# Attention stages of a streaming encoder on one core: sample values once per pair of heads, query squares one head at a time, and the weight split at the pair's end

## The reference, cut to what matters

```python
q = (rms_norm(c_q, q_lat_norm[l]) @ w_uq[l]).reshape(B, L, N_HEADS, QK_DIM)      # 16 heads x 96
q = jnp.concatenate([q[..., :NOPE_DIM], apply_rope(q[..., NOPE_DIM:], pos)], axis=-1)
q = rms_norm(q, q_head_norm[l])
k_nope = (ckv_all @ w_uk[l]).reshape(B, T, N_HEADS, NOPE_DIM)
k = rms_norm(jnp.concatenate([k_nope, kr_all (broadcast to heads)], axis=-1), k_head_norm[l])
v = (ckv_all @ w_uv[l]).reshape(B, T, N_HEADS, V_DIM)
att_out = blocked_attention(q, k, v, pos, k_pos)        # chunk-causal softmax(q k') v
mixed = sigmoid(g_rec) * rec_out + sigmoid(g_att) * att_out
```

## Time and profile before

| | |
|---|---|
| median of 3 runs | 3244.86 us (3240.8 to 3248.27) |
| the profiled execution | 3247.03 us, its span 3245.3 us |
| mean granted TensorE clock | 0.91 of full speed |
| attention, layer 0 and layer 1 | about 430 to 740 us and 1925 to 2245 us of the span |
| DMA, all queues | 119 GB/s over the span |

### The profile page before, as it was taken

One profiled execution on the slowest core, in us unless ns is written; L12 is line 12 of the kernel. 1 busy time (PEld: TensorE's weight loads), 2 busy tenths in 40 slices (PEclk: granted clock), 3 DMA queues, 4 the chain that ended last, 5 costly groups with the idle time before them and its releaser, 6 DMA issues.

```text
span 3245.3 us, 43898 instructions
## 1 busy us (share of the span) xinstructions
PE 2862.5 (88%) x18152; PEld 2624.5 (81%) x18152; DVE 2019.5 (62%) x3294; ACT 1380.2 (43%) x1938; POOL 315.7 (10%) x457
## 2 busy tenths in 40 slices
PE   2998789999798999999789969998888969999996
PEld 2988678888787999999789958887877958888884
DVE  4666666664554443434577567665545368988997
ACT  1334156553333221212333336654333347777773
POOL 3000023330000000000000023221000010000001
PEclk9999789887788999999899979888879889999998
DMA  4322200002131222222122210001212179999995
GB/s 134 124 66 65 56 17 17 9 26 68 65 104 65 65 79 79 78 79 78 59 65 66 65 28 21 11 1 67 91 63 94 66 278 381 384 386 392 384 380 190
DMA packets 219143, 385.28 MB, mean 119 GB/s; under 512 B 34486, under 2 KB 156406, under 8 KB 218944
## 3 DMA queue, kind: packets, MB, share of 16 engines
q1 hardware_dynamic: 202640, 329.80, 28.7%
q0 software_dynamic: 16304, 52.66, 4.6%
HBM read 352.99 MB, written 29.44 MB: 118 GB/s over the span
## 4 chain that ended last, share of the span: by engine, by line
PE 69%; DVE 19%; ACT 8%; issue 2%; DMA 1%; POOL 1%; DVEq 0%; ACTq 0%; POOLq 0%
PE ACC L433 19%; PE ACC L435 18%; PE ACC L434 18%; PE TP L433 3%; PE TP L434 2%; PE TP L435 2%; DVE TR L1574 2%; DVE WL L1363 2%; DVE XC L1541 1%; ACT P L1139 1%; PE TP L905 1%; PE TP L607 1%; DVE PTL L1391 1%; PE ACC L627 1%; PE TP L616 1%
## 5 line engine op out<-in xcount | busy, mean ns | idle before, releaser
L433 PE MATMUL ACC<-XH,WH 128*128 128x288 f32 x1984 | 595.7, 300 | 40.0 <-DVE XP L1442 36.7
L435 PE MATMUL ACC<-XH,WL 128*128 128x288 f32 x1984 | 596.2, 301 | 0.0
L434 PE MATMUL ACC<-XL,WH 128*128 128x288 f32 x1984 | 594.8, 300 | 0.0
L2040 DVE TENSOR_TENSOR WL<-MW,WH 128x2048 fp32r<-128x2048 f32 x192 | 436.9, 2289 | 76.6 <-ACT WH L1297 76.6
L958 ACT ACTIVATE WH<-RAW 128x2048 fp32r<-128x2048 f32 (+1 forms) x129 | 238.0, 1845 | 523.5 <-PE ACC L435 515.5
L1297 ACT ACTIVATE WH<-MW 128x2048 fp32r<-128x2048 f32 x192 | 368.0, 1918 | 145.4 <-PE ACC L435 93.1
L433 PEld LDWEIGHTS ACC<-XH,WH 128*128 128x128 f32 x1984 | 381.0, 192 | 43.4 <-DVE WL L1363 43.1
L434 PEld LDWEIGHTS ACC<-XL,WH 128*128 128x128 f32 x1984 | 380.9, 192 | 0.0
L435 PEld LDWEIGHTS ACC<-XH,WL 128*128 128x128 f32 x1984 | 379.4, 191 | 0.0
L1363 DVE TENSOR_TENSOR WL<-RAW,WH 128x2048 fp32r<-128x2048 f32 (+1 forms) x129 | 284.0, 2202 | 103.0 <-ACT WH L958 102.5
L433 PE MATMUL ACC<-YH,WH 128*128 128x288 f32 x864 | 260.5, 302 | 28.1 <-DVE YL L1914 14.5
(11 more groups left out here) (488 smaller groups left out, 6429.6 us busy)
## 6 DMA issues: line engine op xcount, KB each, us to landing
MW<-in_moe_w_dram SPq DMA_DIRECT2D x192, 1024.0 KB, 7.2
RAW<-in_w_in_dram SPq DMA_DIRECT2D x36, 1024.0 KB
RAW<-in_ffn_w_dram SPq DMA_DIRECT2D x30, 1024.0 KB
dispatched<-ZT POOLq DMA_DIRECT2D x4, 2048.0 KB, 17.8
RAW<-in_w_out_dram SPq DMA_DIRECT2D x8, 1024.0 KB
RAW<-in_w_mk_dram SPq DMA_DIRECT2D x8, 1024.0 KB
RAW<-in_w_mv_dram SPq DMA_DIRECT2D x8, 1024.0 KB
RAW<-in_w_mq_dram SPq DMA_DIRECT2D x8, 1024.0 KB
```

The lines of the kernel that those rows point to most:

```text
L433: nc.tensor.matmul(out, a[0], b[0], start=first, stop=False)
L434: nc.tensor.matmul(out, a[0], b[1], start=False, stop=False)
L435: return nc.tensor.matmul(out, a[1], b[0], start=False, stop=last)
L2040: v.tensor_tensor(low, MW[raw_place(PLACE[key])][:].rearrange("p j n -> p (j n)"), high.bitcast(F32), ALU.subtract)\
```

## The change

The 64 sample columns of both heads of a pair go into one tile (`PSH`, `PSL` become 128 columns wide), and the 15 sample products are made once a pair, 128 columns wide, after the prompt values of the odd head, in a bank `pvs` of its own (`sample_values`). The query squares of a head get a bank each. Those of the even head go between the two halves of the next odd queries; those of the odd head go into the next pair, behind the first group of keys, and VectorE computes an inverse root for each head by itself (`query_means`, `one_scale`) instead of one for both. The third group of keys moves ahead of the turned probabilities. ScalarE and VectorE follow: `keys_out(0)` earlier, `queries_squared(even+2)` ahead of `divided(odd)`, `head_output(even)` ahead of `key_roots`, and the weight split from the even half to just before `keys_high(even+2)` and `keys_low(even+2)`. `PSL` and the second square tile move into unused ends of the weight slots. For the last two pairs of a layer there is no weight split in either kernel; for the last no queries and no keys of a next pair.

```diff
 # attention_order
+        b += [("qs", odd)] if p else []
-        b += [("t", even, n) for n in range(4)] + [("pv", even, n) for n in range(2)]
+        b += [("t", even, n) for n in range(4)] + [("pv", even)]
         b += [("t", odd, n) for n in range(4)]
-        b += [("qs", p + 1)] + [("kt", even + 2, n) for n in range(3)] if more else []
-        b += [("pv", odd, n) for n in range(2)]
+        b += [("qs", even + 2)] if more else []
+        b += [("kt", even + 2, n) for n in range(3)] if more else []
+        b += [("pv", odd), ("pvs", p)]
 # TensorE
+                def sample_values(pair):
+                    emptied_b(*(("t", 2 * pair + j, 1) for j in range(2)))
+                    bank = bank_b(("pvs", pair))
                     for k in (1, 2, 3, 4, 0):
...
-                        mm = product(bank[:, 0:NEW], ...
+                        mm = product(bank[:, 0:2 * NEW], ...
...
-                        keys_and_values(wkv, p + 1, (0, 1))
+                        keys_and_values(wkv, p + 1, (0,))
+                    if p:
+                        query_squares(odd)
+                    if more:
+                        keys_and_values(wkv, p + 1, (1, 2))
                     turn_first(even)
                     turn_second(even)
-                    if more:
-                        keys_and_values(wkv, p + 1, (2,))
                     scores(odd)
...
-                        queries(wq, odd + 2)
-                        query_squares(p + 1)
+                        bank = bank_a(("q", odd + 2))
+                        query_half(wq, odd + 2, bank, 0)
+                        query_squares(even + 2)
+                        query_half(wq, odd + 2, bank, 1).then_inc(s["a_ready"], 1)
                         turn_keys(even + 2)
                     weighted_values(odd)
+                    sample_values(p)
 # ScalarE, even half, then odd half
                     softmax(even)
+                    keys_out(p + 1, 0)
+                    keys_high(odd)
+                    divided(even)
                     mixed_high(p - 1)
-                    divided(even)
-                    keys_high(odd)
-                    keys_out(p + 1, 0)
-                    if p + 2 < PAIRS:
-                        split_high(UA)
...
                     softmax(odd)
+                    queries_squared(even + 2)
                     divided(odd)
-                    queries_squared(even + 2)
                     queries_high(even + 2)
...
                         queries_high(odd + 2)
+                    if p + 2 < PAIRS:
+                        split_high(UA)
                         keys_high(even + 2)
 # VectorE
                     reciprocals_second(even)
+                    if p:
+                        query_means(odd)
+                        one_scale(odd)
+                    keys_low(odd)
                     mixed_low(p - 1)
-                    keys_low(odd)
                     first_low(even)
-                    if p + 2 < PAIRS:
-                        split_low(UA)
                     second_low(even)
...
+                    head_output(even)
                     key_roots()
-                    head_output(even)
...
                     second_low(odd)
+                        query_means(even + 2)
+                        one_scale(even + 2)
                         queries_scaled(odd + 2)
                         queries_low(odd + 2)
-                        query_scales(p + 1)
+                    if p + 2 < PAIRS:
+                        split_low(UA)
                         keys_low(even + 2)
                     head_output(odd)
+                    sample_output(p)
+                def one_scale(head):
+                    at0, q0 = head % 2 * TT, 24 + 16 * (head % 2)
+                    rsqrt(TT, nwt[:, :, at0:at0 + TT])
+                    step(v.tensor_scalar(sm[:, q0:q0 + TT], nwt[:, 2, at0:at0 + TT], QK ** -0.5, None, ALU.mult))
```

More of the change, by code:

```diff
@@ L174, in attention_order @@
     a = [("kv", 0, g) for g in range(3)] + [("q", 0), ("q", 1)]
-    b = [("qs", 0)] + [("kt", 0, n) for n in range(3)]
+    b = [("qs", 0), ("qs", 1)] + [("kt", 0, n) for n in range(3)]
     for p in range(PAIRS):
@@ L314, in stream_step_kernel @@
         KTH, KTL = put("KTH", [P, KEYS], F32R), put("KTL", [P, KEYS], F32R)
-        QSQ = [put("QSQ0", [P, T]), at("QSQ1", [P, T], F32, WL0 - 4 * (UNIT - UA))]
+        QSQ0 = put("QSQ0", [P, T])
+        QSQS = [(QSQ0, slot_end("QSQ1%d" % k, [P, T], F32, 1 - k)) for k in range(DEPTH)]
         AO = put("AO", [P, T])
@@ L589, in keys_and_values, with query_half @@
                         mm.then_inc(s["a_ready"], 1)
+                def query_half(wq, head, bank, h):
+                    cols = slice(h * HALF, (h + 1) * HALF)
+                    for c in range(3):
+                        mm = product(bank[:, h, 0:HALF], (wq[0][:, c, head % 2, :], wq[1][:, c, head % 2, :]),
+                                     (CQH[:, c, cols], CQL[:, c, cols]), c == 0, c == 2)
+                    return mm
                 def queries(wq, head):
                     bank = bank_a(("q", head))
[L593 to L598, removed]
+                    query_half(wq, head, bank, 0)
+                    query_half(wq, head, bank, 1).then_inc(s["a_ready"], 1)
                 def turn_keys(head):
@@ L609, in turn_keys, with query_squares @@
                         mm.then_inc(s["b_ready"], 1)
[L611 to L617, removed]
+                def query_squares(head):
+                    bank = bank_b(("qs", head))
+                    pe.wait_ge(s["q_sq"], layer * N_HEADS + head + 1)
+                    for tt in range(TT):
+                        mm = nc.tensor.matmul(bank[0:rows(tt), tt:tt + 1], QSQS[layer][head % 2][0:QK, tt * P:tt * P + rows(tt)],
+                                              ones[0:QK, 0:1], start=True, stop=True)
                     mm.then_inc(s["b_ready"], 1)
@@ L667, in weighted_values @@
                         pe.wait_ge(s["v_lo"], layer * PAIRS + head // 2 + 1)
-                    emptied_b(*(("t", head, n) for n in range(4)))
-                    bank = bank_b(("pv", head, 0))
+                    emptied_b(*(("t", head, n) for n in (0, 2, 3)))
+                    bank = bank_b(("pv", head))
                     for j in range(4):
@@ L1066, in values_high @@
                     if pair:
-                        act.wait_ge(s["b_ready"], layer * len(B_AT) + B_AT["pv", 2 * pair - 1, 1] + 1)
+                        act.wait_ge(s["b_ready"], layer * len(B_AT) + B_AT["pvs", pair - 1] + 1)
                     fn(key_tiles(VH, 0, 6), VF(0, 6), ACT.Copy)
@@ L1749, in reciprocals_second, with gated, sample_output @@
                     v.reciprocal(sm[:, 34:36], sm[:, 18:20]).then_inc(s["r23"], 1)
+                def gated(tile, half, cols, n, src):
+                    mine = slice(half * 64, half * 64 + 64)
+                    return v.scalar_tensor_tensor(out=AO[mine, cols], in0=TGA[mine, tile, cols], scalar=1.0, in1=TP[mine, n % 4, src],
+                                                  op0=ALU.add, op1=ALU.mult)
                 def head_output(head):
-                    tile, mine = head // 2, slice(head % 2 * 64, head % 2 * 64 + 64)
-                    for k, (cols, width) in enumerate(((slice(0, SEQ), SEQ), (slice(SEQ, T), NEW))):
-                        n = layer * len(B_AT) + B_AT["pv", head, k]
-                        dve.wait_ge(s["b_ready"], n + 1)
-                        v.scalar_tensor_tensor(out=AO[mine, cols], in0=TGA[mine, tile, cols], scalar=1.0, in1=TP[mine, n % 4, 0:width],
-                                               op0=ALU.add, op1=ALU.mult).then_inc(free_b(n), 1)
+                    n = layer * len(B_AT) + B_AT["pv", head]
+                    dve.wait_ge(s["b_ready"], n + 1)
+                    gated(head // 2, head % 2, slice(0, SEQ), n, slice(0, SEQ)).then_inc(free_b(n), 1)
+                def sample_output(pair):
+                    n = layer * len(B_AT) + B_AT["pvs", pair]
+                    dve.wait_ge(s["b_ready"], n + 1)
+                    gated(pair, 0, slice(SEQ, T), n, slice(0, NEW))
+                    gated(pair, 1, slice(SEQ, T), n, slice(NEW, 2 * NEW)).then_inc(free_b(n), 1)
                 def gated_sum(tile):
-                    n = layer * len(B_AT) + B_AT["pv", 2 * tile + 1, 1]
+                    n = layer * len(B_AT) + B_AT["pvs", tile]
                     dve.wait_ge(free_b(n), n // 4 + 1)
```

45 lines of the change are left out of this document (26 added, 19 removed).

## The result

| | before | after |
|---|---|---|
| median | 3246.57 us (4 runs, 3240.8 to 3251.56) | 3300.08 us (4 runs, 3291.18 to 3301.69) |
| profiled execution, its span | 3247.03, 3245.3 us | 3301.69, 3300.0 us |
| twelve `gated_sum` intervals | 491.4 us | 536.7 us |
| mean granted clock of the span | 0.91 | 0.907 |

The ratio is 1.0162 (95%: 1.014 to 1.0184). The sign was predicted, the size was not: 3300 lies 40.6 us above the 3259.5 and outside the range.

What follows compares the result with a forecast made beforehand. It took a ring of VectorE and ScalarE steps, with TensorE filling in, as the bound. 3247.0 + 31.4 of chain - 17 of clock = 3261.5, or 3259.5 us on the median's scale; range 3233 to 3279.

Steps and rivals of the forecast that it cites:

- The sign: The whole kernel gets slower, a change of +0.45%; slower was given a chance of 0.56.
- +31.4: Sum of the longer chain at equal clock over both layers, +15.7 us a layer.
- What is removed: Fifteen sample matmuls a pair, 1.91 us of TensorE; the gain turns into a wait and counts 0.
- Rival D: The wide sample matmuls cost double, +1.9 us in each of 16 pairs, 3290 us; chance 0.03.
- Even half: Odd head's squares ahead of the odd scores delay VectorE's taking them: +0.54 us a pair, up to +1.
- Odd half: The split moved ahead of `keys_low` starts it later: +1.9 us a pair, bounds 0 and 2.7.
- The wait before the sample values: TensorE waits on `KTL` 2 us or more in pairs 0 to 5, below 1 in pair 6.
- What the clock gives back: Of 28 us lost to lower clock in the attention stages, 17 are gained: 6 plus 11, half of 22.
- the falls behind the squares: Clock falls after the query squares, 0.4 to 0.5 us each, 6 us in all, counted as gone.
- C: The clock falls stay as dear as before: +31.4 us, 3276 us; chance 0.12.
- A: TensorE stays the bound and the split costs nothing: sixteen pairs -22 us, 3223 us; chance 0.20.
- B: The clock falls go altogether: +3.4 us, 3248 us, no difference; chance 0.22.

Runs made afterwards that it cites:

- experiment 5: Kernel before with only the sample values made once a pair, squares, roots and split as before: 3225.64 us, ratio 0.995.
- experiment 1: Kernel after with only the weight split put back in the even half: 3267.2 us, ratio 1.0063.
- Experiment 3: Kernel after with 22 dense unused matmuls filling TensorE's wait ahead of the sample values: 3271.32 us, ratio 1.0089.
- experiment 6: Kernel before with only the query squares and roots placed head by head as in the kernel after: 3266.18 us, ratio 1.0071.
- experiment 2: Kernel after with only the even head's inverse root moved behind `keys_low`: 3283.89 us, ratio 1.0119.
- experiment 4: Kernel before with only the weight split moved late, ahead of the next even keys' high and low parts: 3264.25 us, ratio 1.0061.
- experiment 8: Kernel before with a pair's roots behind `keys_low` and VectorE's split ahead of both even low parts: 3231.06 us, ratio 0.9957.
- experiment 10: Kernel before with sample values once a pair, roots behind `keys_low` and VectorE's split ahead of both even low parts: 3203.83 us, ratio 0.9862.

## Why the prediction was right in sign and wrong in size

In the twelve intervals the full-clock sums are 503.8 against 468.3, +35.5 us; the measured difference is 45.3, so the clock makes +9.8. Of the 9.4 us outside, the first pair of a layer is 2.5 us longer at full clock and the last some 0.5, 6 in both layers; what is left, 3, I put to the clock, since the stages outside the pairs differ by only 0.5 us here. Together about +42 us of chain and +13 of clock, against +31.4 and -17 predicted: the chain was 10 too short, the clock 30 too good.

- **What is removed**, right. The wide sample values cost 1.91 us, and taking the 15 narrow ones out leaves the pair at 39.06 (experiment 5). Rival D is out.
- **Even half**, right in kind and nearly in size: +0.74 instead of +0.54. In pair 6 I had +1.1 for the even half, because I made that half of the kernel before 0.55 shorter there; it is 0.1 (24.04 against 24.14 in experiment 5), the even half is +0.8, and the odd half adds 0.6 that I had at nothing: +1.4 (40.40 against 38.97). The first odd maximum now waits for TensorE (0.94 us at 540.35), as predicted.
- **Odd half**, right in kind, +2.53 instead of +1.9. The split itself is the 1.9 (14.66 against 12.77 without one). Another 0.5 (12.77 against 12.25) is in the root and the low parts, whose reordering I had called even: they now run while GpSimd assembles the keys, and single steps of the root take 0.35 us instead of 0.17 and `queries_low` 0.99 instead of 0.76. The last 0.1, from `keys_low` to the scores, I did not trace.
- **The wait before the sample values**, right in kind: on `KTL`, 3.2 us in layer 0 where 2 or more was said (1.7 to 3.2 in layer 1). In pair 6 it is 1.3 and 0.3, where below 1 was said.
- **What the clock gives back**: this step failed. It took 6 us for the falls behind the squares and half of 22 for the rest, 17 in all. It gave nothing back, and the clock took some 13 us more. Cutting up the squares did not end the falls behind them: layer 0 has none (at 531.26 and 552.50 the squares ran at full clock), but in layer 1 five falls begin in or within 1.5 us behind the even head's squares, and experiments 1, 3 and 6 have them too. And a new fall came with the longer wait, in front of the next even scores, where each lost microsecond delays the exponentials. In the pair of 561.70 it costs 564.38 - 561.70 - 1.93 = 0.75 us in the sample values and more in the scores. Each of the twelve pairs with a split has a fall that begins between the end of its odd prompt values and 1.3 us into the next even scores. In layer 0 they begin between 1.4 us ahead of the sample values and 1.7 us behind their start. In pair 6, with the short wait, the sample values stay at 1.00 and a fall begins 0.9 us (layer 0) or 1.9 us (layer 1) into the scores. Experiment 3 shows the wait as the cause by filling it: 29 us come back although TensorE has more to do. Shorter waits than 3 us go with falls too: 2.4 us in experiment 2, up to 2.2 in experiment 4. And experiments 5 and 6 show that I had also put the gift in the wrong place: the falls go with the values, once a pair (23 to 0.4), much less with the squares (23 to 18). That the values have this effect is shown; why is open.
- Of the rivals, C (falls as dear as before, 3276) came nearest and was still 24 us short. The rule behind it, in the Trainium skill (TensorE: Matmul & The Clock Gate, HAM oscillation), that idle gaps between bursts of matmuls bring the clock down, agrees with this trace: in the pair of 561.70 it is 1.00 through 3.1 us of idle, 0.69 and 0.50 behind it, and 1.00 in the same place once the gap is filled. My argument against it was that the falls of the kernel before came without idle time. Both kinds of fall stand in these traces, and the one doesn't exclude the other.
- A: TensorE was never the bound of the changed kernel (86% busy in a stage that got longer, with the wait of 3.2 us on `KTL` in each of layer 0's pairs with a split). B: the falls did not go.

The change holds one gain (values once a pair, -16 us by itself), one large loss (squares and roots by head, +25, nearly all chain), and a second one (the split late, +19 by itself and about +33 on top of the others, there mostly clock: 26 of 31 us in the twelve intervals). The three don't add up: by themselves they come to +28, together to +54.

Open: whether it is the width of the sample values or their place (none in the even half any more) that keeps the clock up in experiment 5; why falls come with no idle time ahead, as in the earlier trace rows, where both the squares and the turned keys stand ahead of the first one and no run parts the two; and why the early split cost clock in the trace of experiment 8 and gave some back in that of experiment 10.

## What to carry to other kernels

When a chain sets the pace, look first for work in it whose result is wanted late (here a root that stood ahead of the low parts of the keys), and move that; moving work into it can cost its full duration (VectorE's 1.4 us of the split in experiment 4, though ScalarE's 1.27 stayed hidden there). A gain in granted clock should be written down with what stands ahead of the dear stretches after the edit: a wait there that grew from at most 0.8 to some 3 us came with a clock cost of 33 us where it had been 23. And try the parts of a change one by one, since here one of three was worth keeping.

## What the hardware showed that I had not expected

- A fall of the granted clock need not show inside the idle stretch that it goes with. Of the six waits of 3.2 us in layer 0, two have it inside (from 514.88 and 695.79, 1.4 us ahead of the work), and four behind, 0.7 to 1.7 us into the work, as in the pair of 561.70. So a fall is to be looked for on both sides of the gap's end.
- VectorE and GpSimd slow each other. In the kernel after, `queries_low` (both operands in SBUF) takes up to 994 ns where GpSimd's assembly of the keys runs beside it and 757 to 760 elsewhere, and the root's small steps with two operands 352 ns or more instead of 165. GpSimd's last instruction in this pair ends just when the steps are short again:

```profile
554.31 0.43 POOL L2247 TENSOR_TENSOR KA<-rp,RK 128x144 f32<-128x144 f32 x1
554.71 0.43 POOL L2248 TENSOR_TENSOR KA<-rp,RK 128x144 f32<-128x144 f32 x1
```

  In the kernel before it is GpSimd that is held: `queries_low` keeps its 757 to 760 ns also beside GpSimd, and the GpSimd instruction that it meets takes 0.97 us instead of 0.43:

```profile
501.61 0.44 POOL L2203 TENSOR_TENSOR KA<-rp,RK 128x144 f32<-128x144 f32 x1
502.01 0.97 POOL L2204 TENSOR_TENSOR KA<-rp,RK 128x144 f32<-128x144 f32 x1
```

  `queries_scaled`, with one operand in PSUM, kept its 0.76 us beside GpSimd. The Trainium skill (SBUF — State Buffer, SBUF: two separate sides) says that a VectorE instruction with two operands in SBUF and a GpSimd instruction that reads SBUF hold the same ports in turn; the trace agrees.
- 22 dense matmuls without use made a kernel 29 us faster than the same kernel without them.
